# Two page tiles ahead of the last norm turn, recent tokens turned before the last page quarter, and the prompt's chunk sums as four column tiles

## The chip, the cores and the metric

One core of one Trainium2 chip runs the whole step in one launch. The metric is device microseconds of an execution; the time before is the median of three executions.

## What is computed

One inference step of a two-layer decoder. Layer 0 is a gated short convolution, layer 1 a native sparse attention (NSA); each also attends into 256 memory tokens. A prompt of 512 tokens and eight samples of 8 new tokens (each with 2,048 cached tokens in 16 pages of 128) share the weights. What bears on the change:

```python
def layer(x, i):
    h = rmsnorm(x, norm_g[i])
    parts = split(h @ w_in[i])
    y = concat(silu(mg) * mem_attend(mq, mem_kv), silu(zg) * mix)
    return x + y @ w_out[i]

def blocks(kv, pos_w, phi):                      # compressed keys and values
    part = einsum('bcjsgd,smjd->mbcsgd', chunks_of_16(kv), pos_w)   # m = 0, 1
    blk = part[0][:, :-1] + part[1][:, 1:]       # block n = chunk n and chunk n+1
    return einsum('bnsgd,sde->bnsge', blk, phi)

def nsa(q, kvc, kvs, kvw, gates):
    o_c, p = attend(q, blocks(kvc))              # compressed
    o_s = attend(q, top 16 blocks of 64 by p)    # selected
    o_w = attend(q, last 512 tokens)             # window
    return gates[0] * o_c + gates[1] * o_s + gates[2] * o_w
```

For the samples `kvc` is the cached page rows, for the prompt the 512 projected rows. All is float32.

## The kernel before, in words

Every engine has its own hand-written program; semaphores tie them together. Three places matter here.

**The NSA norm and projection.** The cached pages are reduced to chunk sums in 32 *page tiles* of four pages (`page_tile`, lines 1802 to 1822): VectorE (DVE) multiplies a 128x2048 tile by two weight tiles (lines 1811, 1812) and adds halves twice (1814 to 1822). The pages come by DMA, issued by SP (`load_pages`, line 579) into two buffers, so that tile T's pages are asked for when tile T-2's second multiply is done (`cp_b`). Sixteen tiles go beside the convolution, four beside its output projection, tiles 20 to 31 here. TensorE (PE) adds each pair of tiles with four 32-column products (`page_sums`, called after an odd tile), at fixed places in its list of work `NSA_WORK`: 21 after piece 2, 23 after piece 5, 25 after piece 7, 27, 29 and 31 after pieces 9, 12 and 15. Pieces 0 to 4 use one weight block, 5 to 8 the next, which SP asks for at line 553 when the output projection is done. The normed rows of the five token tiles are turned on PE (`tile_turns(7)` to `(11)`) and taken into HT by DVE (`take_next`, line 1781). `tile_turns(11)` stands after piece 2 on PE; DVE takes 9, 10 and 11 and only then begins tile 20. Piece 4 is the first to read what `take_next(11)` writes. Before its page loads SP issues one copy of 8,064 KB from DRAM to DRAM, the eight samples' window buffers (line 618).

**The prompt's chunk sums** (PE lines 1543 on). Rows weighted for m = 0 (PA, DVE lines 2028, 2029) and m = 1 (PB, GpSimd/POOL lines 779, 780) are made per token tile p, in two buffers each, so p = 2 waits until the sums of p = 0 are done. PE adds each pair into one 32-row result with two products (`sums`); ACT copies 31 rows (line 1051), PE transposes them (`turn_blocks`), ACT copies again (1053), `phi` follows (756 us), then attention. DVE scatters the samples' queries into QZ (line 2018) before PA; POOL may begin PB once the memory attention is gated.

**The samples' attention.** For each sample, `front` turns ten 128x512 groups of keys on PE into banks 6 and 7, j = 0 to 9; the letters of `FRONT = "AAADADDAAA"` say whether ACT (lines 1128, 1131) or DVE (2134) copies group j. Groups 0 to 7 are the four page quarters, two each, 8 and 9 the window (recent tokens). Quarter c waits for its pages (`sa_lo`, `sa_hi`; SP and POOL issue two pages each, line 535), the window for `sa_w`. Quarters 1 to 3 have two buffers, so they are asked for when the sample two before has used them. On ACT the exponent of the sample before (`exps_sel`, line 1154, 2112 columns) stands between the copies j = 4 and j = 7. `middle` (scores) waits for all ten copies; `back` turns probabilities and multiplies by values, its first copy on ACT at line 1165.

Of the kernel before, what the change touches and what calls it, by code (L numbers as in the profile page):

```python
# [74 lines left out]
FRONT = "AAADADDAAA"  # L75
CONV_TILES = 16
# [140 lines left out]
def build(nc, I, O):  # L217
    ctx = ExitStack()
    with ctx:
# [92 lines left out]
        PA = [at(10240 + 512 * n, 512) for n in range(2)]  # L312
        PB = [at(8192 + 512 * n, 512) for n in range(2)]
# [397 lines left out]
        def _(pool):  # L711
# [61 lines left out]

            for p in range(PT):
                pool.wait_ge(ms_done, 2)
                pool.wait_ge(roped, 4)
                if p >= 2:
                    pool.wait_ge(cp_sum, PAGE_TILES // 2 + p - 1)
                nc.gpsimd.tensor_tensor(heads(PB[p % 2][:, 0:256]), heads(P1[2][:, p, 256:512]), row_pos("pos1", 0), ALU.mult)
                nc.gpsimd.tensor_tensor(heads(PB[p % 2][:, 256:512]), heads(P1[3][:, p, 0:256]), row_pos("pos1", 1),  # L780
                                        ALU.mult).then_inc(cp_rb, 1)
# [26 lines left out]
        def _(act):  # L808
# [242 lines left out]
            nc.scalar.copy(CRp[0:NCP, :], PS[0:NCP, 2, :]).then_inc(cp_rows, 1)  # L1051
# [71 lines left out]
            def front(t, prev):  # L1123
                def took(first, last):
                    for j in range(first, last):
                        act.wait_ge(sa_ft, t.value(10, j + 1, base=START.sa_ft))
                        if j < 8:
                            nc.scalar.copy(skv(t.at(1), j // 2)[:, 2 * (j % 2):2 * (j % 2) + 2, 0:256],  # L1128
                                           PS[:, 6 + j % 2, :].rearrange("p (q c) -> p q c", q=2)).then_inc(sa_fa, 1)
                        else:  # L1130
                            nc.scalar.copy(SWKT[:, j - 8, :], PS[:, 6 + j % 2, :]).then_inc(sa_fa, 1)
# [45 lines left out]
        def _(pe):  # L1177
# [66 lines left out]

            def sums(A, Bp, p, tiles, per, name, out):


                n, o = per * tiles, per * (tiles - 1 - p)
                mm(out, C(name)[:, o:o + n], A, p == 0, False)
                mm(out, C(name)[:, o + 1:o + 1 + n], Bp, False, p == tiles - 1).then_inc(cp_sum, 1)  # L1250

            def turn_blocks(rows, bank, nch):
                for s in range(4):
                    ins = turn(PS[:, bank, 128 * s:128 * s + nch], rows[0:nch, 128 * s:128 * s + 128])
                ins.then_inc(cp_turned, 1)
# [391 lines left out]
            def front(t, prev):  # L1647
# [3 lines left out]
                for j in range(10):  # L1651
                    if j >= 2:
                        pe.wait_ge(sa_fa if FRONT[j - 2] == "A" else sa_fd, front_value(t, j - 2))
                    if j < 8:
                        if j % 2 == 0:
                            places = 2 if j else 3
                            pe.wait_ge(sa_lo[j // 2][number % places], 32 * (number // places + 1))
                            pe.wait_ge(sa_hi[j // 2][number % places], 32 * (number // places + 1))
                        for q in range(2):
                            for g in range(2):  # L1660
                                ins = turn(PS[:, 6 + j % 2, 256 * q + 128 * g:256 * q + 128 * g + 128],
                                           skv(number, j // 2)[:, 2 * (j % 2) + q, 128 * g:128 * g + 128])
                    else:
                        if j == 8:
                            pe.wait_ge(sa_w[number % 3], 16 * (number // 3 + 1))
                        for p in range(4):
                            ins = turn(PS[:, 6 + j % 2, 128 * p:128 * p + 128], SWI[number % 3][:, p, 128 * (j - 8):128 * (j - 7)])
# [94 lines left out]
        def _(dve):  # L1762
# [30 lines left out]
            for r in range(2):  # L1793
                for tp in range(2):
                    for m in range(2):
# [3 lines left out]
                        ins = tcopy(SEL[r][p:p + 32, first + skip:first + 32], ident[p:p + 32, p + skip:p + 32])  # L1799
            ins.then_inc(sel_set, 1)  # L1800
# [213 lines left out]
            dve.wait_ge(r_turned, 11)  # L2014
            for g in range(KVH):
# [8 lines left out]

            for p in range(PT):
                if p >= 2:
                    dve.wait_ge(cp_sum, PAGE_TILES // 2 + p - 1)
                tt(heads(PA[p % 2][:, 0:256]), heads(P1[2][:, p, 256:512]), row_pos("pos0", 0), ALU.mult)
                tt(heads(PA[p % 2][:, 256:512]), heads(P1[3][:, p, 0:256]), row_pos("pos0", 1), ALU.mult
                   ).then_inc(cp_ra, 1)  # L2030


# [97 lines left out]
            def front(t, prev):  # L2130
                n = t.n % 2
                def took(j):
                    dve.wait_ge(sa_ft, t.value(10, j + 1, base=START.sa_ft))
                    tcopy(skv(t.at(1), j // 2)[:, 2 * (j % 2):2 * (j % 2) + 2, 0:256], PS[:, 6 + j % 2, :].rearrange("p (q c) -> p q c", q=2)  # L2134
                          ).then_inc(sa_fd, 1)
# [234 lines left out]
```

## Time and profile before

| | us |
|---|---|
| median of 3 runs (lowest, highest) | 1127.64 (1126.96, 1134.62) |
| the profiled execution, its span | 1138.11, 1136.4 |
| PE busy in the span | 1022.7 (90%) |
| DVE busy | 589.0 (52%) |
| ACT busy | 309.2 (27%) |
| POOL busy | 71.1 (6%) |

The span is cut by the order of the work: convolution to 280 us, memory attention and output projection to 417, the NSA projection to 680, memory attention to 735, the prompt's attention to 885, the samples to 1063, the last projection to the end. A stage's limit is read from the waits of PE in it: who released PE, and how long it had been idle. PE's lines 1179 and 1182 are the helpers through which all its products and transposes go.

### The profile page before, as it was taken

The numbers are of one execution on the slowest core, as the hardware profiler recorded it, in microseconds if no ns is written. First come the engines' busy times: TensorE is split into PE (matmuls) and PEld (weight loads), VectorE is DVE, ScalarE is ACT, GpSimd is POOL, SyncE is SP. The second block draws the span as 40 slices with busy tenths as digits, with TensorE's granted clock in tenths as the row PEclk, the third lists the DMA queues.
The fourth block names the chain that finished last, engine by engine and source line by source line (L and its number), as shares of the span: only waits on it lengthen the run. The fifth ranks groups of instructions, "written<-read, shape, count | busy, mean of one in ns | idle before, by whom it ended". The sixth has DMA issues, their size and how long they took to land.

```text
span 1136.4 us, 17586 instructions
## 1 busy us (share of the span) xinstructions
PE 1022.7 (90%) x6558; PEld 627.7 (55%) x6558; DVE 589.0 (52%) x1326; ACT 309.2 (27%) x749; POOL 71.1 (6%) x124
## 2 busy tenths in 40 slices
PE   6999999999779994999999997778999798899897
PEld 3567677777544451577465465535555564565443
DVE  2207879776435636899000005247885465656113
ACT  4310000000420230111102115236776443543101
POOL 0000000000000000000000005120000112110000
PEclk9999999999969997999999987687999999999899
DMA  8623565453514366564221102430002857765202
GB/s 319 213 61 125 157 185 155 103 151 111 187 38 111 120 252 203 167 170 127 74 74 74 37 1 75 142 96 0 1 1 71 301 191 252 282 211 183 95 1 83
DMA packets 45727, 147.79 MB, mean 130 GB/s; under 512 B 8393, under 2 KB 20170, under 8 KB 38858
## 3 DMA queue, kind: packets, MB, share of 16 engines
q1 hardware_dynamic: 40522, 129.89, 36.2%
q0 software_dynamic: 5120, 16.78, 4.3%
q8 instruction: 52, 0.85, 0.3%
q14 instruction: 33, 0.27, 0.1%
HBM read 139.63 MB, written 15.27 MB: 136 GB/s over the span
## 4 chain that ended last, share of the span: by engine, by line
PE 69%; DVE 14%; DMA 6%; issue 5%; ACT 3%; SPq 1%; POOLq 1%; POOL 0%; DVEq 0%; ACTq 0%
PE PS L1179 60%; PE PS L1182 9%; DMA arena<-in_csel 3%; DVE arena L1811 2%; DVE arena L1812 2%; DVE arena L2077 1%; DMA arena<-in_cmem 1%; DMA arena<-in_ccmp 1%; DVE arena L2096 1%; DMA arena<-in_wall 1%; DVE arena L1814 1%; DVE arena L1901 1%; DVE arena L1781 1%; DVE arena L1891 1%; DVE arena L1820 1%
## 5 line engine op out<-in xcount | busy, mean ns | idle before, releaser
L1179 PE MATMUL PS<-arena 128*32 128x64 f32 (+16 forms) x5460 | 864.7, 384 | 48.2 <-DVE arena L1822 18.6
L1179 PEld LDWEIGHTS PS<-arena 128*128 128x128 f32 (+5 forms) x5460 | 497.7, 153 | 393.2 <-issue 258.1
L1182 PE MATMUL PS<-arena 128*128 128x128 f32 (+3 forms) x1098 | 174.5, 303 | 58.0 <-ACT arena L830 11.1
L1182 PEld LDWEIGHTS PS<-arena 128*128 128x128 f32 (+3 forms) x1098 | 131.2, 153 | 107.5 <-issue 48.0
L1811 DVE TENSOR_TENSOR arena<-arena 128x2048 f32<-128x2048 f32 x32 | 73.2, 2288 | 9.7 <-DMA arena<-in_ccmp 8.5
L1812 DVE TENSOR_TENSOR arena<-arena 128x2048 f32<-128x2048 f32 x32 | 73.1, 2285 | 0.0
L2007 DVE SCALAR_TENSOR_TENSOR arena<-arena 128x576 f32<-128x576 f32 x8 | 5.8, 757 | 127.7 <-ACT arena L1003 127.5
L1084 ACT ACTIVATE arena<-arena 128x512 f32<-128x512 f32 (+3 forms) x96 | 52.9, 554 | 22.8 <-DVE arena L2077 22.8
L2077 DVE CUSTOM_DVE_ANT_0 arena<-PS,arena 128x512 f32<-128x512 f32 (+3 forms) x96 | 41.3, 486 | 20.0 <-PE PS L1179 20.0
L535 POOL DMA_DIRECT2D arena<-in_csel x64 | 34.6, 541 | 240.7 <-PE PS L1182 112.1
L1970 DVE TENSOR_TENSOR arena<-arena,PS 128x512 f32<-128x512 f32 x16 | 11.0, 687 | 58.6 <-PE PS L1179 58.6
L1020 ACT COPY arena<-PS 128x512 f32<-128x512 f32 x16 | 9.4, 587 | 115.4 <-PE PS L1179 115.4
L1814 DVE TENSOR_TENSOR arena<-arena 128x1024 f32<-128x1024 f32 x32 | 39.0, 1218 | 0.0
L1816 DVE TENSOR_TENSOR arena<-arena 128x1024 f32<-128x1024 f32 x32 | 39.0, 1218 | 0.0
L1781 DVE TENSOR_TENSOR arena<-PS,arena 128x512 f32<-128x512 f32 x28 | 17.4, 682 | 39.8 <-PE PS L1182 39.8
L1093 ACT COPY arena<-PS 128x512 f32<-128x512 f32 x60 | 31.9, 580 | 10.0 <-PE PS L1182 10.0
L2205 DVE COPY arena<-PS 128x512 f32<-128x512 f32 (+1 forms) x24 | 15.5, 648 | 28.2 <-PE PS L1182 28.2
L2096 DVE TENSOR_SCALAR arena<-arena 128x128 f32<-128x128 f32 (+1 forms) x96 | 29.5, 383 | 0.4
L1128 ACT COPY arena<-PS 128x512 f32<-128x512 f32 x40 | 22.7, 587 | 22.0 <-PE PS L1182 22.0
L2134 DVE COPY arena<-PS 128x512 f32<-128x512 f32 x24 | 16.6, 693 | 17.4 <-PE PS L1182 17.3
L1011 ACT ACTIVATE arena<-PS 128x384 f32<-128x384 f32 x10 | 4.9, 492 | 71.6 <-PE PS L1179 71.6
L740 POOL MEMSET arena<- 64x2048 f32 x1 | 1.8, 1801 | 331.4 <-ACT arena L876 331.4
(182 smaller groups left out, 540.1 us busy)
## 6 DMA issues: line engine op xcount, KB each, us to landing
arena<-in_wall SPq DMA_DIRECT2D x20, 2048.0 KB, 9.4
arena<-in_ccmp SPq DMA_DIRECT2D x128, 256.0 KB, 3.9
arena<-in_csel SPq DMA_DIRECT2D x64, 256.0 KB, 5.6
arena<-in_csel POOLq DMA_DIRECT2D x64, 256.0 KB, 5.8
arena<-in_cmem SPq DMA_DIRECT2D x32, 256.0 KB, 3.9
arena<-in_win SPq DMA_DIRECT2D x8, 1024.0 KB, 9.6
out_win_s<-in_win SPq DMA_DIRECT2D x1, 8064.0 KB
arena<-in_xp SPq DMA_DIRECT2D x1, 2048.0 KB, 17.0
```

Of the source, the lines that this page charges most:

```text
L535: eng.dma_start(skv(t, c)[:, s, :], I["csel"][bass.ds(page, 1), :, :].rearrange("a p c -> (a p) c")).then_inc(loaded[c][t % places], 16)
L1084: ins = nc.scalar.activation(S, S, ACT.Exp, bias=unit_stats(u, "max")[:, c:c + 1], scale=-1.0, accum_out=unit_stats(u, "sum")[:, c:c + 1])
L1093: nc.scalar.copy(PT_[u % 2][:, 512 * b:512 * b + 512], PS[:, p_bank("turns", g), :]).then_inc(pa_ca, 1)
L1179: return nc.tensor.matmul(out, lhsT, rhs, start=start, stop=stop, skip_group_check=True)
L1182: return nc.tensor.transpose(out, in_, ident[0:in_.shape[0], 0:in_.shape[0]])
L1781: ins = tt(dst[:, 4 * half:4 * half + 4, :], PS[:, bank, :].rearrange("p (k c) -> p k c", k=4), bc(g[:, 4 * half:4 * half + 4], 128), ALU. ...
L1811: tt(tile_view(made[0]), tile_view(PG[T % 2]), tile_pos("tile_pos0"), ALU.mult).then_inc(cp_a, 1)
L1812: tt(tile_view(made[1]), tile_view(PG[T % 2]), tile_pos("tile_pos1"), ALU.mult).then_inc(cp_b, 1)
L1814: tt(made[0][:, 0:1024], made[0][:, 0:1024], made[0][:, 1024:2048], ALU.add).then_inc(cp_half, 1)
L1816: tt(made[1][:, 0:1024], made[1][:, 0:1024], made[1][:, 1024:2048], ALU.add).then_inc(cp_half, 1)
L2077: ins = causal_add(SP[u % 3][:, 1280 * gg + o:1280 * gg + o + nk], PS[:, score_bank(x, gg), 0:nk], FUT[:, 512 - nk:512], 1.0, 3e38, ALU.ad ...
L2096: ins = ts(S, S, w[:, 4 * gg + ti:4 * gg + ti + 1], None, ALU.mult)
```

## The change

1. DVE takes turns 9 and 10, makes page tiles 20 and 21, and then takes turn 11.
2. `TURNED` gives the order in which `front` turns its groups: the window's two at j = 6 and 7, the last quarter's two at j = 8 and 9. Engines, banks and `FRONT` stay.
3. The prompt's PA and PB get four buffers each. POOL makes all four PB without waits between them, but begins only after the queries are turned (`r_turned` 11), since two of the buffers lie over the queries. DVE makes all four PA before the scatter into QZ. PE waits for all of them and sums with eight products of 32 columns, each token tile p into its own 32 partitions. ACT copies 128 rows; the add of the four partial tiles is done by a product with `SELP`, a 128x31 selection made by four small copies at the start, in place of the transpose. PE waits for the scatter only before the attention.

```diff
+TURNED = (0, 1, 2, 3, 4, 5, 8, 9, 6, 7)
...
-        PA = [at(10240 + 512 * n, 512) for n in range(2)]
-        PB = [at(8192 + 512 * n, 512) for n in range(2)]
+        PA = [at(10240 + 512 * n, 512) for n in range(4)]
+        PB = [at(o, 512) for o in (8192, 8704, 12288, 12800)]
+        SELP = stats[:, 349:349 + NCP]
...
+            pool.wait_ge(ms_done, 2)
+            pool.wait_ge(roped, 4)
+            pool.wait_ge(r_turned, 11)
             for p in range(PT):
-                pool.wait_ge(ms_done, 2)
-                pool.wait_ge(roped, 4)
-                if p >= 2:
-                    pool.wait_ge(cp_sum, PAGE_TILES // 2 + p - 1)
-                nc.gpsimd.tensor_tensor(heads(PB[p % 2][:, 0:256]), ...
+                nc.gpsimd.tensor_tensor(heads(PB[p][:, 0:256]), ...
...
-            nc.scalar.copy(CRp[0:NCP, :], PS[0:NCP, 2, :]).then_inc(cp_rows, 1)
+            nc.scalar.copy(CRp, PS[:, 2, :]).then_inc(cp_rows, 1)
...
-            for p in range(PT):
-                pe.wait_ge(cp_ra, NB * NTL + p + 1)
-                pe.wait_ge(cp_rb, NB * NTL + p + 1)
-                sums(PA[p % 2], PB[p % 2], p, PT, 8, "chunk", PS[0:8 * PT, 2, :])
+            pe.wait_ge(cp_ra, NB * NTL + PT)
+            pe.wait_ge(cp_rb, NB * NTL + PT)
+            for shift, part in enumerate((PA, PB)):
+                for p in range(PT):
+                    o = 8 * (PT - 1 - p) + shift
+                    ins = mm(PS[32 * p:32 * p + 32, 2, :], C("chunk")[:, o:o + 32], part[p], shift == 0, shift == 1)
+            ins.then_inc(cp_sum, PT)
             pe.wait_ge(cp_rows, 2 * NB + 1)
-            turn_blocks(CRp, 3, NCP)
+            for s in range(4):
+                ins = mm(PS[:, 3, 128 * s:128 * s + NCP], CRp[:, 128 * s:128 * s + 128], SELP)
+            ins.then_inc(cp_turned, 1)
...
+            pe.wait_ge(r_spread, 6)
...
-                    if j < 8:
-                        if j % 2 == 0:
+                    k = TURNED[j]
+                    if k < 8:
+                        if k % 2 == 0:
...
+            for p in range(4):
+                ins = tcopy(SELP[32 * p:32 * p + 32, :], ident[32 * p:32 * p + 32, 32 * p:32 * p + NCP])
...
-            for j in (9, 10, 11):
-                take_next(j)
-            for T in range(CONV_TILES + OUT0_TILES, PAGE_TILES):
+            take_next(9)
+            take_next(10)
+            page_tile(CONV_TILES + OUT0_TILES)
+            page_tile(CONV_TILES + OUT0_TILES + 1)
+            take_next(11)
+            for T in range(CONV_TILES + OUT0_TILES + 2, PAGE_TILES):
                 page_tile(T)
...
             dve.wait_ge(r_turned, 11)
+            for p in range(PT):
+                tt(heads(PA[p][:, 0:256]), heads(P1[2][:, p, 256:512]), row_pos("pos0", 0), ALU.mult)
+                tt(heads(PA[p][:, 256:512]), heads(P1[3][:, p, 0:256]), row_pos("pos0", 1), ALU.mult).then_inc(cp_ra, 1)
             for g in range(KVH):
...
-            for p in range(PT):
-                if p >= 2:
-                    dve.wait_ge(cp_sum, PAGE_TILES // 2 + p - 1)
-                tt(heads(PA[p % 2][:, 0:256]), ...
...
-                    tcopy(skv(t.at(1), j // 2)[...], PS[:, 6 + j % 2, :]...).then_inc(sa_fd, 1)
+                    k = TURNED[j]
+                    if k < 8:
+                        tcopy(skv(t.at(1), k // 2)[...], PS[:, 6 + j % 2, :]...).then_inc(sa_fd, 1)
+                    else:
+                        tcopy(SWKT[:, k - 8, :], PS[:, 6 + j % 2, :]).then_inc(sa_fd, 1)
```

## Rows read from the trace of the kernel before

**Rows 1.** Timeline, 405 to 480: start us, us, engine line op, [idle before <-releaser].
```profile
434.23 1.29 DVE L1781 TENSOR_TENSOR arena<-PS,arena 128x512 f32<-128x512 f32 x2 [16.02 <-PE PS L1182]
435.44 2.28 DVE L1811 TENSOR_TENSOR arena<-arena 128x2048 f32<-128x2048 f32 x1
...
457.92 2.29 DVE L1811 TENSOR_TENSOR arena<-arena 128x2048 f32<-128x2048 f32 x1 [6.43 <-DMA arena<-in_ccmp]
```

**Rows 2.** Timeline of PE, at sums 21, 23 and 29.
```profile
451.64 1.94 PE L1179 MATMUL PS<-arena 128*32 128x512 f32 x8 [17.01 <-DVE arena L1822]
...
474.14 1.07 PE L1179 MATMUL PS<-arena 128*32 128x512 f32 x8 [0.25 <-DVE arena L1822]
...
522.74 37.60 PE L1179 MATMUL PS<-arena 128*32 128x512 f32 x171 [1.37 <-DVE arena L1822]
```

**Rows 3.** Waits of PE, 880 to 1064: us in total, times, longest us.
```profile
PE PS L1182 <- DMA arena<-in_csel: 7.2, 6, 2.4
```

**Rows 4.** Timeline, fronts of the fourth and sixth samples: PE at quarter 3, ACT.
```profile
950.09 1.06 PE L1182 MATMUL PS<-arena 128*128 128x128 f32 x8 [2.42 <-DMA arena<-in_csel]
...
992.10 1.06 PE L1182 MATMUL PS<-arena 128*128 128x128 f32 x8 [0.43 <-DMA arena<-in_csel]
...
947.60 2.06 ACT L1154 ACTIVATE arena<-arena 128x2112 f32<-128x2112 f32 x1
...
953.60 0.59 ACT L1165 COPY arena<-PS 128x512 f32<-128x512 f32 x1 [0.32 <-PE PS L1182]
...
991.59 2.06 ACT L1154 ACTIVATE arena<-arena 128x2112 f32<-128x2112 f32 x1
...
995.60 0.59 ACT L1165 COPY arena<-PS 128x512 f32<-128x512 f32 x1
```

**Rows 5.** Timeline of SP's DMA issues, 370 to 450.
```profile
399.55 0.86 SPq L618 DMA_DIRECT2D out_win_s<-in_win  x1
...
408.58 0.36 SPq L553 DMA_DIRECT2D arena<-in_wall  x1
```

**Rows 6.** DMA queue, 425 to 435: packets, MB, share of 16 engines.
```profile
q1 hardware_dynamic: 32, 2.06, 47.7%
```

**Rows 7.** Lines 579 (380 to 530) and 553 (300 to 560): time to landing.
```profile
DMA to landing us min/median/max: 2.8/4.1/13.3
...
DMA to landing us min/median/max: 8.1/11.4/45.2
```

**Rows 8.** Windows: length, busy (x) per engine, then granted PE clock, DMA share, GB/s.
```profile
451.60:457.00 5.40, 5.36 (x12) 1.74 (x13) 0.00 (x0) 0.00 (x0) 0.00 (x0) 0.51 0.76 181
...
755.00:764.10 9.10, 5.72 (x39) 3.69 (x39) 3.84 (x18) 4.55 (x16) 2.33 (x4) 1.00 0.45 140
...
774.40:784.60 10.20, 8.04 (x42) 4.57 (x42) 8.83 (x35) 8.56 (x31) 0.00 (x0) 0.83 0.00 1
```

**Rows 9.** Timeline, 718 to 768, the prompt's chunk sums.
```profile
734.21 0.64 POOL L779 TENSOR_TENSOR arena<-arena 128x256 f32<-128x256 f32 x1 [11.29 <-DVE arena L1952]
...
742.38 2.07 DVE L2018 TENSOR_SCALAR arena<-PS 64x64 f32<-64x64 f32 x12 [8.25 <-PE PS L1182]
...
745.80 7.01 PE L1179 MATMUL PS<-arena 128*32 128x512 f32 x12 [3.31 <-issue]
...
748.22 0.43 DVE L2028 TENSOR_TENSOR arena<-arena 128x256 f32<-128x256 f32 x1 [1.84 <-PE PS L1179]
...
748.56 0.86 DVE L2029 TENSOR_TENSOR arena<-arena 128x256 f32<-128x256 f32 x1
749.10 0.82 POOL L780 TENSOR_TENSOR arena<-arena 128x256 f32<-128x256 f32 x1
...
755.52 0.43 PE L1182 MATMUL PS<-arena 31*128 31x31 f32 x4 [0.67 <-ACT arena L1051]
```

**Rows 10.** Line 735, POOL's small copy: ns min/median/max of six.
```profile
L735 POOL COPY arena<-arena x6: 198/2197/2198, 51.1 to 226.3; 128x16 f32<-128x16 f32 x6
```

**Rows 11.** Timeline, 8 to 54: DVE after its set-up copies.
```profile
27.58 0.17 DVE L1770 TENSOR_SCALAR arena<-arena 128x5 f32<-128x5 f32 x1 [9.19 <-ACT arena L818]
```

More of the change, by code:

```diff
@@ L1126, in took @@
                         act.wait_ge(sa_ft, t.value(10, j + 1, base=START.sa_ft))
-                        if j < 8:
-                            nc.scalar.copy(skv(t.at(1), j // 2)[:, 2 * (j % 2):2 * (j % 2) + 2, 0:256],
+                        k = TURNED[j]
+                        if k < 8:
+                            nc.scalar.copy(skv(t.at(1), k // 2)[:, 2 * (k % 2):2 * (k % 2) + 2, 0:256],
                                            PS[:, 6 + j % 2, :].rearrange("p (q c) -> p q c", q=2)).then_inc(sa_fa, 1)
                         else:
-                            nc.scalar.copy(SWKT[:, j - 8, :], PS[:, 6 + j % 2, :]).then_inc(sa_fa, 1)
+                            nc.scalar.copy(SWKT[:, k - 8, :], PS[:, 6 + j % 2, :]).then_inc(sa_fa, 1)
                 if prev is not None:
@@ L1243, in _ @@
             pe.wait_ge(chunk_taken, C0_BLOCKS)
[L1245 to L1255, printed above, removed]
             def phi(BL, bank, nch):
@@ L1653, in front @@
                         pe.wait_ge(sa_fa if FRONT[j - 2] == "A" else sa_fd, front_value(t, j - 2))
-                    if j < 8:
-                        if j % 2 == 0:
-                            places = 2 if j else 3
-                            pe.wait_ge(sa_lo[j // 2][number % places], 32 * (number // places + 1))
-                            pe.wait_ge(sa_hi[j // 2][number % places], 32 * (number // places + 1))
+                    k = TURNED[j]
+                    if k < 8:
+                        if k % 2 == 0:
+                            places = 2 if k else 3
+                            pe.wait_ge(sa_lo[k // 2][number % places], 32 * (number // places + 1))
+                            pe.wait_ge(sa_hi[k // 2][number % places], 32 * (number // places + 1))
                         for q in range(2):
@@ L1661, in front @@
                                 ins = turn(PS[:, 6 + j % 2, 256 * q + 128 * g:256 * q + 128 * g + 128],
-                                           skv(number, j // 2)[:, 2 * (j % 2) + q, 128 * g:128 * g + 128])
+                                           skv(number, k // 2)[:, 2 * (k % 2) + q, 128 * g:128 * g + 128])
                     else:
-                        if j == 8:
+                        if k == 8:
                             pe.wait_ge(sa_w[number % 3], 16 * (number // 3 + 1))
                         for p in range(4):
-                            ins = turn(PS[:, 6 + j % 2, 128 * p:128 * p + 128], SWI[number % 3][:, p, 128 * (j - 8):128 * (j - 7)])
+                            ins = turn(PS[:, 6 + j % 2, 128 * p:128 * p + 128], SWI[number % 3][:, p, 128 * (k - 8):128 * (k - 7)])
                     ins.then_inc(sa_ft, 1)
@@ L2133, in took @@
                     dve.wait_ge(sa_ft, t.value(10, j + 1, base=START.sa_ft))
-                    tcopy(skv(t.at(1), j // 2)[:, 2 * (j % 2):2 * (j % 2) + 2, 0:256], PS[:, 6 + j % 2, :].rearrange("p (q c) -> p q c", q=2)
-                          ).then_inc(sa_fd, 1)
+                    k = TURNED[j]
+                    if k < 8:
+                        tcopy(skv(t.at(1), k // 2)[:, 2 * (k % 2):2 * (k % 2) + 2, 0:256],
+                              PS[:, 6 + j % 2, :].rearrange("p (q c) -> p q c", q=2)).then_inc(sa_fd, 1)
+                    else:
+                        tcopy(SWKT[:, k - 8, :], PS[:, 6 + j % 2, :]).then_inc(sa_fd, 1)
                 def cmp_max():
```

7 lines of the change are left out of this document (2 added, 5 removed).

## The prediction, made blind

> **What bounds the kernel now.** The table gives PE 90% of the span, so I read first where PE stands still, stage by stage, and then who ends each wait. Three places belong to this change.
>
> In the NSA norm, DVE finishes turn 10 at 418.2 and idles 16.02 us for turn 11, although tile 20 is its next work anyway; tiles 20 and 21 then run from 435.44, and PE, which wants sums 21 right behind turn 11, idles 17.01 us until 451.64 [rows 1, 2]. The reader should also see that this is not the last wait: tile 22 waits 6.43 us for its pages until 457.92 [rows 1], and from there DVE makes a tile each 8.1 us (two of them to sums 23 at 474.14) while PE comes to sums 23 and sums 29 only 0.25 and 1.37 us early [rows 2]. So from 457.92 to 522.74 the two engines are level, DVE just ahead as the bound; behind that PE runs alone.
>
> At the prompt's sums PE waits 3.31 us for the first PA and then works through four double-buffered rounds to the transpose at 755.52 [rows 9]. In the samples PE waits 7.2 us for pages in six fronts, 2.4 at most [rows 3].
>
> **The change part by part.**
>
> *Page tiles.* DVE does tiles 20 and 21 in its idle time: 418.2 + 2 x 8.1 = 434.4, where turn 11 comes at 434.23 now; 0.2 us late, which nobody meets, since the first reader is piece 4. PE's 17 us go: sums 21 start at 434.6. They and pieces 3 to 5 take from 451.64 to 473.89 now (474.14 less 0.25), 22.25 us, of which 5.4 us passed at a granted clock of 0.51 [rows 2, 8], a loss of 5.4 x 0.49 = 2.6; without it 19.6 us, to 454.2. What is late next?
>
> Piece 5 needs the weights asked for at 408.58 [rows 5], which landed 45.2 us later, at 453.8, where the same load takes 8.1 at best [rows 7]. The 8,064 KB copy in front of them moves 2.06 MB in 10 us with under half of the engines' share [rows 6], 40 us in all from its issue at 399.55 [rows 5], so to 440. Weights on the engines that it holds wait until then; now pages of tile 22, asked for when tile 20's two multiplies are done, 435.44 + 2 x 2.28 = 440.0 [rows 1], compete with them. After the change those pages are asked for at 418.2 + 4.6 = 422.8, and stand in the same queue behind the weights. I estimate the weights at 447 (440 and most of 8.1) and the pages one page load later (2.8 at best [rows 7]), at 450. So PE is through piece 5 at 455 and then waits for tile 23, which ends at 450 + 16.2 = 466.2, 7.9 us earlier than now. That new idle of 11 us stands where the 17 stood, and as after those, I expect 1.2 GHz for the first 5.4 us: 2.6 us lost. DVE would release sums 29 at 522.74 - 7.9 = 514.8; PE would come there at 521.37 (522.74 less 1.37) - 7.9 + 2.6 = 516.1. PE decides: **6.6 us gained**. Bounds: pages no earlier than now, 457.92, leave DVE's chain and add the cold restart, 1.3 slower; pages in the usual 4.1 us [rows 7] give 21 (first rival). I take 450 because the one load seen behind that copy waited for it.
>
> *Chunk sums.* Both engines may start at 742.4 [rows 9]. POOL's eight multiplies (now half of them are done early, from 734.21, behind PE's turns) and DVE's eight meet. Alone a POOL one takes 0.64 and DVE's come 0.34 apart; where they meet, two of each take 1.70 us (748.22 to 749.92), one DVE op 0.86 [rows 9]. Eight pairs at 0.85 are 6.8: PE starts at 749.2 instead of 745.80. The scatter (2.07) moves behind PA, done by 752, before the attention wants it. The sixteen matrix instructions of 32 columns, two per product, are two groups like sums 23 (1.07) or 21 (1.94 at half clock) [rows 2]; after 6.7 us without work I take half clock, 3.9 us, to 753.1. ACT's copy holds PE 0.67 as before, 128 rows or 31. The four products with SELP are eight instructions for the transpose's four at 0.43 [rows 9], 0.9 us, or 1.8 at half clock; I take 1.3, giving 755.1 against 755.95. Of the 0.9 I set 0.4 aside for the clock behind it: **0.5 gained**. Bounds: no meeting and full clock, POOL done at 747.5, the sums at 749.6, SELP's at 751.2, 4.8 gained; each op alone in turn (0.98 a pair, 750.2, 756.6 after SELP) and the 5.7 us of PE's work until 764.1 at half clock [rows 8], 6.3 lost. Between ends so far apart I stay with the pair's row.
>
> The Trainium skill has a rule against this part (SBUF — State Buffer, Who interferes with whom): a DVE instruction with two SBUF inputs and a GpSimd instruction that reads SBUF exclude each other for the whole instruction. The trace agrees in kind: POOL's copy of 16 columns takes 198 ns or, beside DVE's 2.28 us multiply, 2,197 [rows 10]. By the rule the eight pairs take 8 x 0.98 = 7.8 us, PE starts at 750.2, and this part loses 0.5: the sum would be 1.0 smaller.
>
> *Recent tokens.* The last quarter is wanted two groups later, when its pages are there, and the window has been loaded a sample before. But not all 7.2 us come back. ACT's 2.06 us exponent stands ahead of copy 7, and group 9 waits for copy 7. In the sixth front, with a wait of 0.43, the first copy of back starts 4.01 us after the exponent, with ACT filled from 991.59 on; in the fourth, with 2.42, 6.00 us after it [rows 4]. The difference, 1.99, is 2.42 - 0.43: a wait of 0.43 is hidden. So 7.2 - 6 x 0.43 = 4.6, less 0.5 since the fourth's pages come after even the later place: **4.1 gained**. Bounds: 0, if the wait only moves, and 5.0. The copies keep size, engine and order, so DVE and ACT gain nothing else; loads are triggered by back, so their distance to the front stays.
>
> *SELP's set-up.* Four small copies on DVE near 18.4; DVE then idles 9.19 us for ACT [rows 11]. Nothing.
>
> Sum: 6.6 + 0.5 + 4.1 = 11.2. The profiled execution took 1138.1 (span 1136.4), so 1126.9 for it; it stands 10.5 above the median, and I apply the sum to that: 1127.64 - 11.2 = 1116.4.
>
> **The rivals.**
>
> *Pages not queued behind the copy.* If tile 22's pages land 4.1 us after issue, DVE never waits, tile 23 is done at 451.9, PE goes from piece 5 on without stop (19.6 us earlier, no cold restart) and reaches sums 29 near 501.7: 21 gained there, 25.6 in all, 1102. For it: half of the engines' share is free [rows 6]. Against: 13.3 us for a page and 45.2 for the weights [rows 7]. The Trainium skill speaks against it as well (DMA: Bandwidth & Descriptors, Why a DMA increments its semaphore by 16 and not by 1, and Queues, rings and completion order): a copy from SP runs on as many engines, up to 16, as divide its outermost dimension, and each engine takes its ring in order; that dimension is 8 samples here, so half of every page would stay behind the copy. By that rule this rival falls; 47.7% in rows 6 agrees with 8 of 16.
>
> *Pages no earlier than now.* The pages compete with the weights on the same engines however early they are asked for, and tile 22 starts at 457.92 still. Sums 23 at 474.14 as now, with PE cold after a longer idle: 1.3 slower there, 3.3 gained in all, 1124.3. For it: the queue's backlog, not the issue, ended tile 22's wait. Against: in the trace they were asked for only at 440.
>
> *The samples' wait only moves.* Quarter 3 is still late at j = 8 and the exponent fixes the rest: 4.1 go, 7.1 remain, 1120.5. For it: the sixth front's hidden 0.43. Against: the waits' mean is 1.2 (7.2 in six), and two groups on PE take 1.06 [rows 4] without the copies between them.
>
> *Slower: the clock at the prompt.* PE's idle before the chunk sums grows from 3.3 to 6.7 us. If TensorE stays at 1.2 GHz from there through the short, broken attention start to 784.6, the 5.7 and 8.0 us of PE's work in stretches now at 1.00 and 0.83 [rows 8] nearly double: 13.7 lost, 2.5 more than all gains, 1130. It decides from 11.2 us, some 11 us of work done cold that is warm now. Against: the clock came back after 5.4 us of work at 457 [rows 8].
>
> *Chunk sums better than set.* POOL and DVE hardly meet and the clock holds: 4.8 there, 15.5 in all, 1112.1. For it: DVE's first op of a pair kept its 0.43 [rows 9]. Against: the second did not.
>
> **How the numbers follow.** A measurement of this kernel tells about 1%, 11.3 us, from no change; my sum lies on that line. Forecast 0.52, its own range 1112 to 1121, split 0.27 below 1116.4 and 0.25 above. Unqueued pages 0.08 and better chunk sums 0.08 are faster by over 1%: 0.43. Pages as now 0.10, the moved wait 0.16 and the clock 0.04 lie within 1%: with 0.25, 0.55. The clock has another 0.02 for coming with one of the other two losses and more, slower by over 1%. The range 1109.5 to 1125.5 leaves out the unqueued pages and the clock, 0.14 together, and tails of the others.
>
> **What would show it.** Right: DVE's idle before turn 11 gone, sums 21 near 434.6, a new PE idle of about 11 us before sums 23 near 466, sums 29 near 516, then the rest shifted by 6.6; no wait on in_csel above 0.5 in the fronts and 4.0 us from exponent to back's first copy; PE's product with SELP near 753.5 and POOL's eight multiplies over 6 to 7.5 us. Wrong: tile 22 at 457 or at 436, sums 23 without a wait, in_csel waits at j = 8, or a granted clock of 0.5 through 755 to 765.

## The result, and the profile after

The changed kernel took 1122.42 us in the median (1116.49 to 1127.12, 19 executions) where the kernel before, run beside it, took 1131.02 (1123.69 to 1138.47, 19 executions). The ratio is 0.9945, with a 95% interval of 0.9927 to 0.9963: 6.2 us faster, between 4.2 and 8.3. The forecast was 11.2. The two medians stand further apart, 8.6 us; why isn't shown, and this text goes by the ratio, which has an interval. The time lies inside the range, and the gain within the 1% that had the chance of 0.55.

The two profiled spans differ by more, 1136.4 against 1123.2, and that 13.2 must not be read as the gain. The profiled execution of the kernel before was one of its longest, and by 405 us, ahead of the first edited stage, the one after is already 2.4 us earlier. Laid side by side by PE's instructions, it wins 3.4 us more from there to the sums of 29, 2.9 from 720 to 795, and 4.4 in the samples. Of the 2.9, 1.2 fall in the query turns, the same fifty instructions ahead of the edit (8.22 us before, 7.02 after, shown below), and are no gain of the change.

The first place. The timelines of DVE, of PE and of SP's DMA issues, of the kernel after, answer to [rows 1, 2, 5]:

```profile
414.56 1.29 DVE L1779 TENSOR_TENSOR arena<-PS,arena 128x512 f32<-128x512 f32 x2 [4.36 <-PE PS L1184]
415.76 2.28 DVE L1811 TENSOR_TENSOR arena<-arena 128x2048 f32<-128x2048 f32 x1
...
431.87 1.29 DVE L1779 TENSOR_TENSOR arena<-PS,arena 128x512 f32<-128x512 f32 x2
450.27 2.29 DVE L1811 TENSOR_TENSOR arena<-arena 128x2048 f32<-128x2048 f32 x1 [17.11 <-DMA arena<-in_ccmp]
...
484.60 2.29 DVE L1811 TENSOR_TENSOR arena<-arena 128x2048 f32<-128x2048 f32 x1 [2.04 <-DMA arena<-in_ccmp]
```

```profile
432.20 11.75 PE L1181 MATMUL PS<-arena 128*32 128x512 f32 x56
446.38 8.03 PE L1181 MATMUL PS<-arena 128*128 128x384 f32 x32 [2.43 <-DMA arena<-in_wall]
466.49 31.02 PE L1181 MATMUL PS<-arena 128*32 128x512 f32 x136 [12.08 <-DVE arena L1822]
...
517.02 3.48 PE L1181 MATMUL PS<-arena 128*32 128x512 f32 x41 [0.69 <-DVE arena L1822]
```

```profile
397.19 0.86 SPq L620 DMA_DIRECT2D out_win_s<-in_win  x1
...
406.22 0.36 SPq L555 DMA_DIRECT2D arena<-in_wall  x1
421.20 45.94 SPq L581 DMA_DIRECT2D arena<-in_ccmp  x16
```

DVE's 16 us ahead of turn 11 are gone and PE starts the sums of 21 behind turn 11 (432.20). But DVE then stands 17.11 us for the pages of tile 22, asked for from 421.20 on, and PE gets two new waits: 2.43 for the weights, 12.08 for tile 23. The 17 us of before have mostly become these.

The prompt's chunk sums, timeline of the kernel after, for [rows 9], from the query turns to the first turns of the samples:

```profile
727.83 7.02 PE L1184 MATMUL PS<-arena 128*128 128x128 f32 x50 [1.09 <-DVE arena L1952]
...
734.74 0.43 DVE L2019 TENSOR_TENSOR arena<-arena 128x256 f32<-128x256 f32 x1 [7.05 <-PE PS L1184]
734.77 0.88 POOL L780 TENSOR_TENSOR arena<-arena 128x256 f32<-128x256 f32 x1 [17.82 <-PE PS L1184]
...
740.29 0.81 POOL L781 TENSOR_TENSOR arena<-arena 128x256 f32<-128x256 f32 x1
...
741.25 3.65 PE L1181 MATMUL PS<-arena 128*32 128x512 f32 x16 [6.40 <-POOL arena L781]
...
745.59 1.08 PE L1181 MATMUL PS<-arena 128*128 128x31 f32 x8 [0.69 <-ACT arena L1052]
...
747.02 1.19 PE L1181 MATMUL PS<-arena 128*128 128x31 f32 x8 [0.36 <-ACT arena L1054]
...
749.57 3.36 PE L1181 MATMUL PS<-arena 64*128 64x512 f32 x8 [1.36 <-ACT arena L1062]
...
876.50 1.06 PE L1184 MATMUL PS<-arena 128*128 128x128 f32 x8 [0.84 <-issue]
```

The same places on PE in the kernel before: query turns, `phi`, first scores, first turns of the samples:

```profile
734.28 8.22 PE L1182 MATMUL PS<-arena 128*128 128x128 f32 x50 [1.09 <-DVE arena L1952]
...
756.31 1.18 PE L1179 MATMUL PS<-arena 128*128 128x31 f32 x8 [0.36 <-ACT arena L1053]
...
758.86 1.77 PE L1179 MATMUL PS<-arena 64*128 64x512 f32 x8 [1.37 <-ACT arena L1061]
...
885.29 1.07 PE L1182 MATMUL PS<-arena 128*128 128x128 f32 x8 [0.84 <-issue]
```

The part itself is shorter: from DVE's start to the end of the product with SELP 11.9 us (734.74 to 746.67), against 13.6 to the end of the transpose before (742.38 to 755.95). But PE idles 6.40 us ahead of it, twice as long as before, and its sixteen instructions take 3.65 us, as at half clock (1.93 in e7, below); the first scores take 3.36, where they took 1.77. Windows of 60 us from the start of the query turns, kernel before and kernel after (length, busy (x) of PE, PEld, DVE, ACT, POOL, granted PE clock, DMA share, GB/s):

```profile
734.30:794.30 60.00, 49.88 (x232) 28.99 (x232) 33.68 (x129) 30.55 (x89) 8.17 (x13) 0.78 0.19 58
```

```profile
727.80:787.80 60.00, 47.43 (x252) 30.21 (x254) 37.43 (x132) 31.50 (x94) 9.07 (x13) 0.74 0.21 61
```

The samples: waits of PE between 859 and 1052, and ACT's timeline in the fronts of the fourth and sixth sample, for [rows 3, 4]:

```profile
PE PS L1184 <- DMA arena<-in_csel: 0.7, 2, 0.4
```

```profile
937.69 2.06 ACT L1156 ACTIVATE arena<-arena 128x2112 f32<-128x2112 f32 x1
...
941.61 0.59 ACT L1167 COPY arena<-PS 128x512 f32<-128x512 f32 x1
...
978.42 2.06 ACT L1156 ACTIVATE arena<-arena 128x2112 f32<-128x2112 f32 x1
...
982.35 0.59 ACT L1167 COPY arena<-PS 128x512 f32<-128x512 f32 x1
```

The wait for pages fell from 7.2 to 0.7, and both fronts show 3.92 to 3.93 us from the exponent to the first copy of back, where the fourth had 6.00.

### The profile page after: what moved, and what is told of

It reads as the page before. It is cut to its first block, busy times and chain, and to the rows that moved or that the text cites. A ratio compares the mean times of both kernels' runs of the same rounds, so it can differ in the third digit from the quotient of the medians.

```text
span 1123.2 us, 17593 instructions
## 1 busy us (share of the span) xinstructions
PE 1017.9 (91%) x6562; PEld 626.6 (56%) x6562; DVE 592.4 (53%) x1330; ACT 307.9 (27%) x749; POOL 71.8 (6%) x124
## 4 chain that ended last, share of the span: by engine, by line
PE 71%; DVE 13%; DMA 7%; ACT 4%; issue 4%; SPq 1%; POOL 1%; POOLq 0%; DVEq 0%; ACTq 0%
PE PS L1181 62%; PE PS L1184 10%; DMA arena<-in_ccmp 3%; DVE arena L1811 2%; DVE arena L1812 2%; DVE arena L2074 1%; DMA arena<-in_csel 1%; DMA arena<-in_cmem 1%; DMA arena<-in_wall 1%; DVE arena L2093 1%; ACT arena L1156 1%; ACT arena L1130 1%; DVE arena L1814 1%; DVE arena L1901 1%; DVE arena L1779 1%
## 5 line engine op out<-in xcount | busy, mean ns | idle before, releaser
L1181 PE MATMUL PS<-arena 128*32 128x64 f32 (+18 forms) x5468 | 863.0, 385 | 46.0 <-DVE arena L1822 12.8
L1181 PEld LDWEIGHTS PS<-arena 128*128 128x128 f32 (+6 forms) x5468 | 499.4, 153 | 386.7 <-issue 247.5
L1184 PEld LDWEIGHTS PS<-arena 128*128 128x128 f32 (+3 forms) x1094 | 128.4, 151 | 101.8 <-issue 40.5
L2074 DVE CUSTOM_DVE_ANT_0 arena<-PS,arena 128x512 f32<-128x512 f32 (+3 forms) x96 | 41.5, 488 | 20.0 <-PE PS L1181 20.0
L1021 ACT COPY arena<-PS 128x512 f32<-128x512 f32 x16 | 9.4, 586 | 95.8 <-PE PS L1181 95.8
L1094 ACT COPY arena<-PS 128x512 f32<-128x512 f32 x60 | 32.0, 579 | 10.5 <-PE PS L1184 10.5
L1130 ACT COPY arena<-PS 128x512 f32<-128x512 f32 x48 | 27.3, 589 | 19.8 <-PE PS L1184 19.4
L1173 ACT ACTIVATE arena<-arena 128x1024 f32<-128x1024 f32 x5 | 5.3, 1057 | 62.4 <-DVE arena L1970 60.1
```

Source lines behind the costliest of these rows:

```text
L1094: nc.scalar.copy(PT_[u % 2][:, 512 * b:512 * b + 512], PS[:, p_bank("turns", g), :]).then_inc(pa_ca, 1)
L1130: nc.scalar.copy(skv(t.at(1), k // 2)[:, 2 * (k % 2):2 * (k % 2) + 2, 0:256], PS[:, 6 + j % 2, :].rearrange("p (q c) -> p q c", q=2)).then ...
L1181: return nc.tensor.matmul(out, lhsT, rhs, start=start, stop=stop, skip_group_check=True)
L1184: return nc.tensor.transpose(out, in_, ident[0:in_.shape[0], 0:in_.shape[0]])
L2074: ins = causal_add(SP[u % 3][:, 1280 * gg + o:1280 * gg + o + nk], PS[:, score_bank(x, gg), 0:nk], FUT[:, 512 - nk:512], 1.0, 3e38, ALU.ad ...
```

## The experiments

All times are medians; each ratio is to the kernel before on the same chip in the same minutes, with a 95% interval. "Clock" is the mean granted clock over all executions of that kernel; "60 us" is the granted clock of the profiled execution in the 60 us from the start of the query turns. Beside e5 to e8, e9 to e11 and e12 the kernel before took 1129.55 (23 executions, clock 0.953), 1130.05 (11, 0.950) and 1129.40 us (11, 0.951), so a mean clock is known to some 0.002.

| kernel | us (executions) | ratio (95%) | clock | 60 us |
|---|---|---|---|---|
| before, beside e1 to e4 | 1128.63 (29) | | 0.953 | 0.78 |
| the change | 1122.42 (19) | 0.9945 (0.9927 to 0.9963) | 0.949 | 0.74 |
| e1 page tiles alone | 1127.06 (12) | 0.9971 (0.9940 to 1.0001) | 0.953 | 0.83 |
| e2 recent tokens alone | 1123.59 (12) | 0.9966 (0.9936 to 0.9996) | 0.953 | 0.81 |
| e3 chunk sums alone | 1131.19 (12) | 1.0023 (0.9995 to 1.0052) | 0.946 | 0.78 |
| e4 change, copy late | 1104.63 (6) | 0.9787 (0.9742 to 0.9831) | 0.956 | 0.72 |
| e5 before, copy late | 1128.16 (12) | 0.9989 (0.9961 to 1.0017) | 0.950 | 0.83 |
| e6 = e4, POOL early | 1102.90 (6) | 0.9751 (0.9708 to 0.9793) | 0.957 | 0.74 |
| e7 = e3, PE kept busy | 1128.40 (12) | 0.9979 (0.9950 to 1.0008) | 0.954 | 0.92 |
| e8 = e4, old chunk sums | 1105.60 (6) | 0.9753 (0.9703 to 0.9804) | 0.961 | 0.85 |
| e9 = e6, PE kept busy | 1098.95 (5) | 0.9724 (0.9701 to 0.9747) | 0.960 | 0.80 |
| e10 = e4, PE kept busy | 1098.69 (5) | 0.9720 (0.9698 to 0.9743) | 0.964 | 0.86 |
| e11 = change, PE kept busy | 1119.71 (6) | 0.9901 (0.9871 to 0.9931) | 0.956 | 0.86 |
| e12 change, copy in 28 rows | 1113.62 (6) | 0.9858 (0.9817 to 0.9899) | 0.952 | 0.77 |

### Each part alone

e1 makes only the first edit on the kernel before:

```diff
-            for j in (9, 10, 11):
-                take_next(j)
+            take_next(9)
+            take_next(10)
+            page_tile(CONV_TILES + OUT0_TILES)
+            page_tile(CONV_TILES + OUT0_TILES + 1)
+            take_next(11)
```

> Only the two page tiles stand ahead of turn 11; samples and prompt as in the kernel before. Theory (the pages of tile 22 stand in the queue behind the 8,064 KB copy): DVE's idle ahead of tile 22 is 17 us, PE waits about 12 us for the sums of 23, and the time falls by 3 to 4 us. Rival (the stage gives the 6.6 us that were forecast, and what the whole change lacks was lost at the prompt): 6 to 7 us. Second rival (PE's new idle only replaces the old one): within 1 us of the kernel before.

Measured: 0.9971, 3.3 us faster (0.1 slower to 6.8 faster), the size of the first theory, though the interval still holds the second rival and barely the first. Here the stages ahead ran as in the profile of before (0.3 us apart), so its DVE and PE timelines compare directly:

```profile
453.08 2.29 DVE L1811 TENSOR_TENSOR arena<-arena 128x2048 f32<-128x2048 f32 x1 [17.91 <-DMA arena<-in_ccmp]
```

```profile
448.76 9.72 PE L1179 MATMUL PS<-arena 128*128 128x384 f32 x32 [2.79 <-DMA arena<-in_wall]
469.30 30.51 PE L1179 MATMUL PS<-arena 128*32 128x512 f32 x136 [10.83 <-DVE arena L1822]
...
518.84 6.39 PE L1179 MATMUL PS<-arena 128*32 128x512 f32 x53 [0.21 <-DVE arena L1822]
```

Tile 22 starts 4.8 us earlier than in [rows 1], the sums of 29 3.9 earlier than in [rows 2]. So 3.6 us are won between turn 11 and the sums of 29, which speaks against the 6 to 7 of the first rival.

e2 makes only the second:

```diff
+TURNED = (0, 1, 2, 3, 4, 5, 8, 9, 6, 7)
...
+                    k = TURNED[j]
-                    if j < 8:
+                    if k < 8:
...
```

> Only the order of the turned groups in the samples is changed. Theory (a wait of 0.4 us is hidden behind the exponent, the rest of the 7.2 us comes back): PE's waits for in_csel fall below 1 us and the time by 4 to 4.5 us. Rival (the wait moves to the copies of the groups that are now last): 2 us or less.

Measured: 0.9966, 3.8 us faster (0.5 to 7.2). In its trace no wait of PE for in_csel is left in the samples, and the seven distances from the exponent to back's first copy are 3.92 to 3.93 us; in the profile of before they ran from 4.01 to 6.00. The theory holds; the rival falls with the waits, since nothing took their place.

e3 makes only the third edit (the diff of the chapter on the change, without its first and second part).

> Only the prompt's chunk sums are changed. Theory (eight pairs of multiplies in 6.4 us, sixteen products at half clock, product with SELP, then the first scores at half clock): 1 to 2.5 us faster. Rival (the clock falls for the whole start of the attention): 2 us slower or more. Rival (the old four rounds cost more than the rows showed): over 4 us faster.

Measured: 1.0023, 2.6 us slower (0.6 faster to 5.9 slower). The theory of a small gain falls by its size; what stands out is the clock, 0.946 in the mean of its 12 executions against 0.953 in the 29 of the kernel before. The time alone doesn't tell it from no change; the clock points to the first rival, and e7 puts that to the test.

### The copy between DRAM regions

e4 is the changed kernel with one line moved:

```diff
-            sp.dma_start(O["win_s"][:, 0:WIN - NT, :], I["win"][:, NT:WIN, :]).then_inc(win_copied, 16)
...
                 load_pages(first, min(first + 4, PAGE_TILES))
+                if n == B_N + 4:
+                    sp.dma_start(O["win_s"][:, 0:WIN - NT, :], I["win"][:, NT:WIN, :]).then_inc(win_copied, 16)
```

> The changed kernel, but the 8,064 KB copy between DRAM regions is issued after the weight load of the fifth block of the NSA projection, when all pages have been asked for. Theory (weights and pages waited in the queue behind that copy): tile 22 starts right behind turn 11, near 433 on the time line, PE goes from the sums of 21 through piece 5 to the sums of 23 without a wait, the sums of 29 start near 501, and the time is 14 to 17 us below the changed kernel's, some 22 below the kernel before. Rival (the pages compete with the weights and with the other loads however the copy stands): tile 22 stays at 445 to 450 and the time within 2 us of the changed kernel. Second rival (the copy only does its harm elsewhere, to weights or memory tokens between 536 and 680): the 15 us come back there as new waits for in_wall or in_cmem.

Measured: 1104.63, ratio 0.9787, 24 us below the kernel before and 17.8 below the changed kernel, a little over what the theory gave. DVE's and PE's timelines of e4:

```profile
428.07 1.29 DVE L1780 TENSOR_TENSOR arena<-PS,arena 128x512 f32<-128x512 f32 x2
429.28 2.28 DVE L1812 TENSOR_TENSOR arena<-arena 128x2048 f32<-128x2048 f32 x1
```

```profile
428.40 48.05 PE L1182 MATMUL PS<-arena 128*32 128x512 f32 x224
477.34 42.89 PE L1182 MATMUL PS<-arena 128*128 128x256 f32 x220 [0.89 <-ACT arena L1014]
```

Tile 22 follows turn 11 without a gap, and one unbroken row of 224 instructions runs from the sums of 21 past those of 23. No wait came back later: behind the copy, issued at 514.31, the next weights (548.91) took 16.1 us to land, where 8.1 is the least in this trace, and PE waited for no weights there.

e5 moves the same line in the kernel before, and nothing else.

> The kernel before, with nothing changed but the place of the 8,064 KB copy (behind the weight load of the fifth block of the NSA projection). Theory (the two edits of this stage need each other): DVE no longer waits 6.4 us for tile 22, but PE still waits 17 us for tile 21 and then needs its 22 us to the sums of 23, so that only PE's small waits of 0.25 and 1.37 us go: 1 to 3 us faster than the kernel before, and the two page tiles are worth some 18 us more on top of it. Rival (tile 22's wait is the bound of the stage): 6 us faster or more.

Measured: 0.9989, 1.2 us faster (4.4 faster to 1.9 slower), so the 6 us of the rival are excluded. PE's timeline of e5:

```profile
449.48 50.59 PE L1180 MATMUL PS<-arena 128*32 128x512 f32 x224 [17.01 <-DVE arena L1823]
500.96 24.25 PE L1180 MATMUL PS<-arena 128*128 128x256 f32 x149 [0.89 <-ACT arena L1013]
```

DVE has no gap at tile 22 any more, and PE's 17.01 us stay whole. The two edits of this stage need each other: the page tiles alone are worth 3.3 us, the late copy alone 1.2, and both together some 23 (e4's 24.0, less the 3.8 of e2, plus the 2.6 of e3; 21.4 by the traces of the stage, below).

e12 leaves the copy in its place and only writes it in another order of dimensions, in the changed kernel:

```diff
-            sp.dma_start(O["win_s"][:, 0:WIN - NT, :], I["win"][:, NT:WIN, :]).then_inc(win_copied, 16)
+            cut = lambda a: a.rearrange("b (h r) c -> h b (r c)", h=28)
+            sp.dma_start(cut(O["win_s"][:, 0:WIN - NT, :]), cut(I["win"][:, NT:WIN, :])).then_inc(win_copied, 16)
```

> The changed kernel with the 8,064 KB copy at its old place, but written as 28 outer rows of 8 samples in place of 8 samples (the same bytes). Theory (the copy takes so long because its eight outer rows keep only half of the DMA engines, 48% of their time, busy): the share rises to 80 to 90% while it runs, it is over 15 us earlier, near 425, tile 22 starts behind turn 11 at 433 to 437 and the time comes near the late copy's, 1104 to 1108. Rival (the bytes or the memory set the copy's time): share as before, tile 22 near 450, time within 2 us of the changed kernel. Second rival (the copy is over earlier, but holds up the loads of the convolution's end or the weights on all engines instead): tile 22 near 440 and 1110 to 1116.

Measured: 1113.62, ratio 0.9858, 8.8 us below the changed kernel (9.8 by the ratios): the second rival. Windows of e12 (columns as above) and its DVE and PE timelines:

```profile
425.00:430.00 5.00, 5.00 (x24) 2.26 (x23) 4.39 (x6) 0.59 (x1) 0.00 (x0) 1.00 1.00 164
...
440.00:445.00 5.00, 5.00 (x24) 3.52 (x21) 5.00 (x4) 0.74 (x2) 0.00 (x0) 1.00 0.03 8
```

```profile
439.09 2.29 DVE L1812 TENSOR_TENSOR arena<-arena 128x2048 f32<-128x2048 f32 x1 [9.65 <-DMA arena<-in_ccmp]
```

```profile
455.30 31.20 PE L1182 MATMUL PS<-arena 128*32 128x512 f32 x136 [7.12 <-DVE arena L1823]
```

The DMA share, 0.48 while the copy ran alone [rows 6], is 0.87 to 1.00 in every 5 us from 395 to 435; the engines are idle by 440, and DVE's wait for tile 22 is 9.65 us in place of 17.11. The copy itself was over when the theory had it: in the trace of e12 its packets, 36,864 bytes each, run mostly 14 at a time and end at 422.49, 29.0 us after its issue; in the kernel before they are of 64,512 bytes, run 8 at a time and end 42.7 us after it. So the copy's eight outer rows did set how much of the DMA engines it used. But the weights behind it landed only at 435.0; what held them for the 12.5 us from the copy's end isn't shown.

The Trainium skill (DMA: Bandwidth & Descriptors, Why a DMA increments its semaphore by 16 and not by 1) has the rule that the number of engines is the largest one up to 16 that divides the outermost dimension, 8 for 8 samples and 14 for 28 rows. The traces agree: 48% of the engines' time is 8 of 16, and the copy's packets run 8 and 14 at a time.

### The clock behind the chunk sums

e7 is e3 with products that nobody reads, in PE's wait ahead of the sums:

```diff
             pe.wait_ge(r_took, 10)
+            for n in range(5):
+                mm(PS[:, 3, :], ident, X[:, n % PT, 0:512])
             pe.wait_ge(cp_ra, NB * NTL + PT)
```

> The chunk sums alone, with five products of 512 columns that nobody reads in PE's wait ahead of the sums. Theory (the longer wait lowers TensorE's clock in what follows, and this eats the gain of the part: mean granted clock 0.946 with the part against 0.953 without): the mean clock of the executions returns to 0.951 or more and the time falls 4 to 6 us below the chunk sums alone, to about 1125. Rival (the part's own path is longer than the profile shows, the clock is not its doing): clock and time within 1 us of the chunk sums alone, or slower by what the five products reach beyond the wait.

Measured: 0.9979 against e3's 1.0023, 5.0 us better (0.4 to 9.6, from the two intervals), and a mean clock of 0.954 against 0.946. By the medians it is 2.8, and 1128.40 where the theory had about 1125. Windows of 60 us, e3 and e7, and e7's PE:

```profile
728.20:788.20 60.00, 45.96 (x256) 28.55 (x256) 37.97 (x133) 31.57 (x95) 9.07 (x13) 0.78 0.20 57
```

```profile
722.80:782.80 60.00, 48.81 (x286) 29.54 (x287) 40.65 (x145) 34.65 (x102) 9.08 (x13) 0.92 0.20 60
```

```profile
729.80 4.56 PE L1181 MATMUL PS<-arena 128*128 128x512 f32 x10 [0.23 <-ACT arena L1048]
735.97 1.93 PE L1181 MATMUL PS<-arena 128*32 128x512 f32 x16 [1.61 <-POOL arena L781]
```

The sixteen instructions take 1.93 us (3.58 in e3), and in the same 60 us DVE and ACT get through 12 and 7 instructions more. PE did more work, and the kernel became faster: PE's idle time ahead of the sums had lowered the clock of the sums and of what follows. The profiled execution is the fastest of its twelve, so its 0.92 is no mean; the table further down has the times of this stage over four such profiles.

e11 does the same in the changed kernel, and e10 in e4.

> The changed kernel with the five unread products in PE's wait ahead of the chunk sums. Theory (that wait costs the clock in what follows, 3 to 5 us): mean granted clock from 0.949 to 0.953 or more, 1118 to 1119 us, 0.989 to 0.991 of the kernel before. Rival (it did so only with the chunk sums alone): within 1 us of the changed kernel, 0.9945.

> The late copy with all three parts and the five unread products. Theory: the mean clock rises from 0.956 towards the 0.961 of the old sums, and the time falls by 3 to 4 us to 1101. Rival: clock and time stay (1104.8).

Measured: e11 0.9901 against 0.9945, 5.0 us better (2.7 by the medians), at a clock of 0.956 against 0.949; e10 0.9720 against 0.9787, 7.6 better by the ratios and 5.9 by the medians, at 0.964 against 0.956. Both go the way of the theory, e10 further than its 3 to 4 us.

The stage itself tells more than the whole times. On PE, from the end of the query turns to `phi`, and from there to the first turns of the samples, means over the profiled executions in us (the sum with its lowest and highest):

| | turns to `phi` | `phi` to samples | sum |
|---|---|---|---|
| old sums: before, e1, e2, e5, e8 | 13.8 | 127.3 | 141.0 (138.8 to 142.8) |
| new sums: the change, e3, e4, e6, e12 | 12.1 | 129.2 | 141.4 (140.8 to 141.7) |
| new sums, PE kept busy: e7, e9, e10, e11 | 10.0 | 127.6 | 137.6 (137.1 to 138.1) |

The new sums win 1.6 us up to `phi` and lose 1.9 behind it. Keeping PE busy wins 3.8 us in the stage, over half of it up to `phi`, where the sixteen instructions run at full clock; e9, with three products, wins its part up to `phi` alone (8.6 and 129.5). Whether the same products would win as much with the old sums, in PE's wait of 3.31 us there, wasn't tried.

e8 is e4 with the prompt's sums of the kernel before.

> The kernel with the late copy, but with the prompt's chunk sums as in the kernel before. Theory (that part alone cost 2.6 us): some 2 to 3 us faster than the late copy with all three parts, 1102, at a higher mean clock. Rival (that part gains its 1 to 2.5 us here): 1106 to 1107.

Measured: 0.9753 against 0.9787, but medians of 1105.60 against 1104.63 with six executions each: inconclusive. In the stage of the table above the two profiles need 142.2 and 141.7 us, so neither the theory's gain nor the rival's loss shows there; the mean clock is higher, 0.961 against 0.956.

e6 lets POOL start early on two of the four token tiles, in e4:

```diff
-            pool.wait_ge(r_turned, 11)
             for p in range(PT):
+                if p == 2:
+                    pool.wait_ge(r_turned, 11)
```

> The kernel with the late copy, and POOL makes the PB of the first two token tiles without waiting for the queries' turns (their buffers do not lie over the queries). Theory (POOL and DVE slow each other where they meet): half of POOL's multiplies are done before DVE starts, PE's wait ahead of the chunk sums falls from 6.4 to about 4.3 us, and the time falls by 2 us or, if the shorter idle also keeps the clock up, by up to 6. Rival (the two engines do not slow each other, DVE's own eight multiplies set the wait): wait of 6 us and no difference.

Measured: 1102.90, 1.7 below e4 by the medians and 4.1 by the ratios, whose intervals don't tell it from nothing. Timelines of e6, POOL early, then DVE alone behind its fourth multiply, and PE:

```profile
708.18 0.64 POOL L782 TENSOR_TENSOR arena<-arena 128x256 f32<-128x256 f32 x1 [10.88 <-DVE arena L1954]
...
717.67 0.86 DVE L2022 TENSOR_TENSOR arena<-arena 128x256 f32<-128x256 f32 x1
...
718.45 0.41 DVE L2021 TENSOR_TENSOR arena<-arena 128x256 f32<-128x256 f32 x1
718.79 0.41 DVE L2022 TENSOR_TENSOR arena<-arena 128x256 f32<-128x256 f32 x1
...
719.97 3.64 PE L1183 MATMUL PS<-arena 128*32 128x512 f32 x16 [4.53 <-DVE arena L2022]
```

PE's wait is 4.53 us, as the theory had it (4.3). DVE's multiplies come 0.78 apart beside POOL's and 0.34 apart without them. The clock did not rise with the shorter wait (0.74 in the 60 us).

e9 adds three unread products to e6.

> The late copy, POOL's early start and three unread products in the 4.5 us that PE still waits. Theory (2 us of shorter path and the warm clock add up): 1099 to 1100, the fastest of all, clock 0.960 or more. Rival (the two overlap, since a shorter wait already keeps part of the clock): 1101 to 1103.

Measured: 1098.95 at a clock of 0.960, the theory's time. But e10 is as fast (1098.69, with nearly the same interval) without POOL's early start: with PE kept busy, that start adds nothing that can be told. e10 and e9 are the fastest versions found, 2.8% below the kernel before.

## Why the prediction was right and wrong

The three forecasts were 6.6, 0.5 and 4.1; the parts alone measured 3.3, -2.6 and 3.8, together 4.5, and the whole change 6.2 (4.2 to 8.3), which agree within their intervals. In the stages of the profiles the parts come to 3.4, about nothing and 4.4. Of the 5.0 us that are missing, 3.3 are the page tiles' and some 0.8 the chunk sums'; the rest can't be told from noise.

*Recent tokens, 4.1: right.* Measured 3.8. "A wait of 0.43 is hidden" held half: of the two waits left in the profile after, the one of 0.29 at 916.17 was hidden (3.92 us from exponent to copy), the one of 0.38 at 997.81 was not (4.65).

*Page tiles, 6.6: right mechanism, mis-sized term.* As forecast, sums 21 follow turn 11, the weights come near 447, tile 22 at 450, PE idles 11 to 12 us ahead of sums 23 near 466, and sums 29 start near 516 (517.02). But that execution ran 2.4 us ahead of the one before from the start, so the same clock times mean less gain. The term that failed is the estimate "weights at 447 and the pages one page load later, at 450", that is 47.5 and 50.5 us behind the issue of the copy at 399.55. Measured from the copy's issue (397.19) they took 49.2 and 53.1 us: 2.6 too few. Most of it is the copy's length: its packets run to 439.51 in the trace, 42.3 us behind the issue, where the sum had 40.5. The pages needed 3.9 us behind the weights, not the best case of 2.8. Another 0.7 is the 2.04 us that DVE waits at 484.60 for the pages of tile 26, asked for behind the next weight load; the prediction had DVE running through there, and PE, otherwise ready 0.69 earlier, now waits for it. 6.6 - 2.6 - 0.7 = 3.3.

*The first rival, unqueued pages.* It failed on its condition, as argued from [rows 6, 7], but its price was right: it gave 21 us in this stage, and e4, which makes the condition true, wins 21.4 there (6.2 us ahead of the profile of before at 434, 27.5 at 525). The obstacle that decided against it was one line away, and e4 shows that it was worth more than all parts of the change.

*Chunk sums, 0.5: near nothing, by a mis-sized term.* The working up to SELP was near: pairs at 0.78 us (forecast 0.85), PE starting 6.5 us behind DVE's start (6.8), half clock for the sums, 1.6 us gained at SELP's end (0.9). The step that failed is "of the 0.9 I set 0.4 aside for the clock behind it". In the profiled executions with the old sums (before, e1, e2, e5, e8) the clock of the 60 us was 0.78 to 0.85, 0.82 in the mean; with the new ones (the change, e3, e4, e6, e12) 0.72 to 0.78, 0.75 in the mean. What this cost is read from the stage: 1.9 us from `phi` to the samples, not 0.4, so that 1.6 won and 1.9 lost leave some 0.3 lost. e3's 2.6 slower holds that in its interval (0.6 faster to 5.9 slower); whether the part loses more than that, these runs can't tell: the five profiles with the old sums spread over 4.0 us in this stage. The slower rival had this mechanism and place, a longer PE idle ahead of the sums, at 13.7 us, some seven times what it came to. The objection against it, that the clock came back after 5.4 us of work at 457, was taken from a stretch where PE then works without a break; here it has breaks all the way to 780. That this is the difference is argued, and wasn't tried.

*The other rivals.* Tile 22 started at 450.27 (452.6 on the time line of before) and not at 457.92, so the pages did come earlier. The samples' wait did not move to another place (e2). POOL and DVE met in all eight pairs, 0.78 us apart, so the better chunk sums, with their 4.8, fell too.

*SELP's set-up, nothing:* no run contradicts it, and none measures it alone.

*The base.* The sum was taken from a median of three executions, 1127.64; with 19 it was 1131.02. Of the 3.4 us between them nothing in the working could tell.

## What to carry to other kernels

When a wait is filled by moving work forward, ask which transfers the moved work will now ask for and what stands ahead of them in the queue: one bulk copy, placed where the DMA had seemed half free, took 18 of some 21 us. Count PE's longest idle stretches in an edit as well as their sum; a shorter path with a longer hole in it can win nothing, and five products that nobody reads, put into the hole, won some 4 us here. And build a ledger of terms from several profiles, or from one part at a time: two executions of one kernel differ by more than each of these terms.

## What the runs showed of the hardware

The times of one kernel's executions go with the clock that they were granted: in the 29 of the kernel before, from 1119.75 to 1135.12 us, a fitted line falls 8.0 us for each 0.01 of mean granted clock (correlation -0.81). The two profiled executions had 0.946 each, where those 29 have 0.953 in the mean and the 19 of the change 0.949; by that line the one before is 5.6 us long and the one after 2.4, so that, as an estimate, 3.2 of the 13.2 between the spans are this chance alone.

POOL and DVE slow each other, but less than by taking turns. The Trainium skill (SBUF — State Buffer, Who interferes with whom) states that such instructions exclude each other for their whole length, by which a pair would cost, as an estimate, 0.98 us (0.34 and 0.64). The trace of the change differs, with eight pairs in 6.36 us (734.74 to 741.10), 0.8 each, and the measurement decides.

The outermost dimension of this DMA decided how much of the DMA engines it held: the same 8,064 KB as 8 outer rows left half of them free and ran to 439.51 with the weights waiting behind it, as 28 rows it ran 14 packets at a time, and the weights behind it landed 41.5 us after its issue (393.46, 32.5 us after their own at 402.50) in place of 49.2. Neither is as good as issuing it where nobody is waiting.
